# Sums as rows spread by one-hot products, outputs by column halves in turn, input copies ahead of the last exponential, in the state space mixer of a hybrid decoder step

## The reference, cut to what matters

```python
acs = jnp.cumsum(dt * a.reshape(G, J), axis=2)
...
seg = acs[:, :, :, None] - acs[:, :, None, :]
decay = jnp.exp(jnp.where(causal, seg, -jnp.inf))
cb = jnp.einsum('bclgn,bcsgn->bclsg', cc, bc)
y_diag = jnp.einsum('bclsg,bclsgj,bcsgjp->bclgjp', cb, decay, xdt)
...
y_off = jnp.einsum('bclgn,bcgjpn,bclgj->bclgjp', cc, starts, jnp.exp(acs))
```

## Time and profile before

| what | value |
|---|---|
| time before, median of 3 runs | 1987.99 us (1986.82 to 1989.16) |
| the profiled execution | 1985.48 us, span of its trace 1983.7 us |
| TensorE busy | 1925.9 us (97%) |
| VectorE, ScalarE, GpSimd busy | 1252.1, 936.9, 1026.3 us |
| granted clock of TensorE, mean | 0.99 |

### The profile page before, as it was taken

How to read it: one execution, slowest core, us unless ns; L and a number is a source line. 1 busy time by engine, 2 the same in 40 slices (tenths; PEclk the granted TensorE clock), 3 DMA queues, 4 the chain that set the end, 5 groups by cost and what they waited for, 6 DMA issues and landing times.

```text
span 1983.7 us, 35763 instructions
## 1 busy us (share of the span) xinstructions
PE 1925.9 (97%) x13954; PEld 1737.1 (88%) x13954; DVE 1252.1 (63%) x2224; ACT 936.9 (47%) x1573; POOL 1026.3 (52%) x1249
## 2 busy tenths in 40 slices
PE   7999999998999999999999999999999999999997
PEld 5999989798888988788889999999997889889976
DVE  5888343426887788764246888888455158874452
ACT  3676522334565555343345455454342347774333
POOL 4787704036456556232337767677550357675602
PEclk8999999999999999999999999999999999999998
DMA  4444476635344444386454444545487344445860
GB/s 136 147 143 151 139 245 234 213 107 176 111 133 133 133 139 148 112 307 213 141 169 151 132 141 146 153 147 162 142 307 244 107 138 147 133 155 177 278 228 27
DMA packets 332615, 324.64 MB, mean 164 GB/s; under 512 B 19768, under 2 KB 313056, under 8 KB 332448
## 3 DMA queue, kind: packets, MB, share of 16 engines
q1 hardware_dynamic: 330944, 321.49, 50.9%
q10 hardware_dynamic: 1504, 0.87, 0.2%
HBM read 292.16 MB, written 29.61 MB: 162 GB/s over the span
## 4 chain that ended last, share of the span: by engine, by line
PE 61%; DVE 9%; ACT 4%; issue 2%; ACTq 0%; DVEq 0%
PE ps L788 9%; PE ps L793 8%; PE ps L789 8%; PE ps L1487 4%; PE ps L1276 3%; PE ps L1496 2%; PE ps L1553 2%; PE ps L778 2%; PE ps L779 2%; PE ps L780 2%; DVE work L2581 2%; PE ps L1631 1%; PE ps L1570 1%; ACT wh L1742 1%; PE ps L1600 1%
## 5 line engine op out<-in xcount | busy, mean ns | idle before, releaser
L1722 POOL TENSOR_TENSOR wl<-raw,wh 128x256 fp32r<-128x256 f32 x1216 | 1020.8, 874 | 929.6 <-ACT wh L1742 929.4
L1742 ACT ACTIVATE wh<-raw 128x1024 fp32r<-128x1024 f32 x304 | 311.6, 1053 | 164.5 <-PE ps L793 61.8
L788 PE MATMUL ps<-Hh,wh 128*128 128x320 f32 x1200 | 366.3, 319 | 2.3 <-DVE work L2601 0.9
L789 PE MATMUL ps<-Hl,wh 128*128 128x320 f32 x1200 | 354.1, 309 | 0.0
L788 PEld LDWEIGHTS ps<-Hh,wh 128*128 128x128 f32 x1200 | 225.3, 188 | 10.9 <-issue 1.9
L789 PEld LDWEIGHTS ps<-Hl,wh 128*128 128x128 f32 x1200 | 225.5, 188 | 2.2
L2296 DVE TENSOR_SCALAR work<-ps 128x512 f32<-128x512 f32 (+8 forms) x220 | 100.4, 474 | 169.7 <-PE ps L886 40.2
L793 PE MATMUL ps<-Hh,wl 128*128 128x320 f32 x1200 | 200.4, 309 | 0.0
L793 PEld LDWEIGHTS ps<-Hh,wl 128*128 128x128 f32 x1200 | 182.1, 188 | 0.1
L788 PE MATMUL ps<-Oh,wh 128*128 128x320 f32 x512 | 152.3, 311 | 3.7 <-DVE Ol L3048 3.7
L789 PE MATMUL ps<-Ol,wh 128*128 128x320 f32 x512 | 151.2, 308 | 0.0
(11 more groups left out here) (446 smaller groups left out, 3899.0 us busy)
## 6 DMA issues: line engine op xcount, KB each, us to landing
raw<-rg_w_in SPq DMA_DIRECT2D x128, 256.0 KB, 3.6
raw<-hg_w_in SPq DMA_DIRECT2D x128, 256.0 KB, 3.6
raw<-ssd_w_in SPq DMA_DIRECT2D x96, 256.0 KB, 4.0
work<-cache_mem_k SPq DMA_DIRECT2D x40, 512.0 KB, 6.2
work<-cache_mem_v SPq DMA_DIRECT2D x40, 512.0 KB, 4.9
raw<-rg_w_out SPq DMA_DIRECT2D x64, 256.0 KB, 3.6
raw<-x_w_k SPq DMA_DIRECT2D x64, 256.0 KB, 3.7
raw<-x_w_v SPq DMA_DIRECT2D x64, 256.0 KB, 3.8
```

Of the source, the lines that this page charges most:

```text
L788: pe.matmul(ps[:, bank, 0:n], high(half, k), mh[:, k, 0:n], start=(k == 0), stop=False)
L789: pe.matmul(ps[:, bank, 0:n], high(half, k), ml[:, k, 0:n], start=False, stop=False)
L1722: ins = pool.tensor_tensor(out, src, wh[:, parted(n) % HALVES, r:r + 2].bitcast(F32), ALU.subtract)
L1742: act.activation(wh[:, nx.n % HALVES], raw[:, slot, :, half * P:(half + 1) * P], ACT.Copy).then_inc(hi_ready, 1)
```

## The change

Once, in `sums_of_steps`, TensorE also makes the running sums as rows: row 32T + head of a new tile `sd_acs` holds the sums of that head in block T. ScalarE copies them out with two more instructions. `decays(j)` then takes the row of one head and spreads it over 128 partitions by a product with a one-hot column of the identity, repeated 128 times. These products have 32 rows, blocks 0, 1 and 2 in rows 0, 32 and 64 of the array; they go head by head with the three blocks in turn, and all waits for the banks stand ahead of the first.

In `outputs` the two products of each head are ordered so that the two column halves (rows 0 to 63 and 64 to 127 of the bank) alternate; the two products of 64 columns follow.

On ScalarE `take_in(i)` moves ahead of the last exponential of `exps`, and the `ahead(u + 3)` between them goes. On VectorE `last_rows` of the group before moves into `conv`, ahead of its last four instructions.

```diff
+        sd_acs = sb("sd_acs", [96, P])
...
                     for T in range(2):
                         pe.matmul(ps[:, 5, 32 * T:32 * T + 32], upper[:], sd_ta[:, 1, T, :], start=True, stop=True)
                         pe.matmul(ps[:, 5, 96 + 32 * T:128 + 32 * T], later[:], sd_ta[:, 1, T, :], start=True, stop=True)
+                        pe.matmul(ps[32 * T:32 * T + 32, 5, 256:384], sd_ta[:, 1, T, :], upper[:], start=True, stop=True)
                     pe.matmul(ps[:, 5, 192:224], ones[:], sd_ta[:, 1, 1, :], start=True, stop=True)
                     pe.matmul(ps[64:P, 5, 64:96], s_causal[64:P], sd_ta[64:P, 1, 2, :], start=True, stop=True)
+                    pe.matmul(ps[64:96, 5, 256:320], sd_ta[64:P, 1, 2, :], s_causal[64:P], start=True, stop=True)
...
                 def decays(j):
-                    def dta(T, h, n, rows=slice(0, P)):
-                        return sd_ta[rows, 1, T, 4 * j + h:4 * j + h + 1].broadcast_to([rows.stop - rows.start, n])
-
-                    for T, bank, read in ((0, 4, "sd_xt_read"), (1, 5, "sd_xs_read")):
-                        pe.wait_ge(*past(read, j + 1))
-                        for h in range(4):
-                            mm = pe.matmul(ps[:, bank, h * P:(h + 1) * P], dta(T, h, P), upper[:], start=True, stop=True)
-                        mm.then_inc(S(f"sd_seg{T}_full"), 1)
+                    pe.wait_ge(*past("sd_xt_read", j + 1))
+                    pe.wait_ge(*past("sd_xs_read", j + 1))
                     pe.wait_ge(*past("sd_bt_read", j + 1))
+                    for h in range(4):
+                        for T in range(3):
+                            rows, w, c = slice(32 * T, 32 * T + 32), (P, P, 64)[T], 32 * T + 4 * j + h
+                            one = ident[rows, c:c + 1].broadcast_to([32, P])
+                            mm = pe.matmul(ps[:, 4 + T, h * w:(h + 1) * w], one, sd_acs[rows, 0:w], start=True, stop=True)
+                            if h == 3:
+                                mm.then_inc(S(f"sd_seg{T}_full"), 1)
                     pe.wait_ge(*past("sd_cb_read", j + 1))
-                    for h in range(4):
-                        mm = pe.matmul(ps[:, 6, h * 64:(h + 1) * 64], dta(2, h, P, sm), s_causal[sm], start=True, stop=True)
-                    mm.then_inc(S("sd_seg2_full"), 1)
...
+                    for T in range(2):
+                        for n in range(2):
+                            h, rows = 2 * t + n, slice(64 * n, 64 * n + 64)
+                            pe.matmul(ps[rows, bank, T * P:(T + 1) * P], sd_xt[:, T, h, :], sd_e[:, T, h, :], start=True, stop=True)
                     for n in range(2):
-                        h = 2 * t + n
-                        rows = slice(64 * n, 64 * n + 64)
-                        for T in range(2):
-                            pe.matmul(ps[rows, bank, T * P:(T + 1) * P], sd_xt[:, T, h, :], sd_e[:, T, h, :], start=True, stop=True)
+                        h, rows = 2 * t + n, slice(64 * n, 64 * n + 64)
                         pe.matmul(ps[rows, bank, 256:320], sd_xt[sm, 2, h, :], sd_e[sm, 2, h, 0:64], start=True, stop=True)
...
                     steps.did(act.activation(w[:, 2, 0:64], ps[:, 5, 0:64], ACT.Copy))
+                    steps.did(act.activation(sd_acs[0:64], ps[0:64, 5, 256:384], ACT.Copy))
+                    steps.did(act.activation(sd_acs[64:96, 0:64], ps[64:96, 5, 256:320], ACT.Copy))
...
                     if j >= 0:
-                        exps(j)
-                    ahead(u + 3)
+                        exps(j, (0, 1, 2), (1, 2))
                     take_in(i)
+                    if j >= 0:
+                        exps(j, (2,), ())
                     ahead(u + 4)
...
                     for k in range(1, 4):
+                        if k == 3 and i:
+                            last_rows(i - 1)
...
                     conv(i)
-                    if j >= 0:
-                        last_rows(j)
                     pack(i)
```

More of the change, by code:

```diff
@@ L1949, in o_high, with exps @@
                     act.activation(Oh[:, o:o + 2, :], sd_y, ACT.Copy).then_inc(S("sd_o_high"), 1)
-                def exps(j):
+                def exps(j, blocks, sums):
                     def of_sums(bank, w, at, n):
@@ L1956, in of_sums @@
                         return act.activation(sd_eo[rows, :, at:at + w], sums, ACT.Exp)
-                    for T in range(3):
+                    for T in blocks:
                         act.wait_ge(*past(f"sd_seg{T}_ready", j + 1))
-                        if T:
+                        if T in sums:
                             steps.did(of_sums(4 + T, (P, 64)[T - 1], (0, P)[T - 1], 0))
                             of_sums(4 + T, (P, 64)[T - 1], (0, P)[T - 1], 1).then_inc(S(f"sd_eo{T}_read"), 1)
+                        if T == 2 and sums:
+                            return
                         rows, w = (slice(0, P), P) if T < 2 else (slice(64, P), 64)
@@ L2044, in ssd @@
                 ahead(u + 2)
-                exps(7)
+                exps(7, (0, 1, 2), (1, 2))
+                exps(7, (2,), ())
                 ahead(u + 3)
```

## The result

The change makes the kernel slower: 1997.27 us (median of 5 runs, 1994.38 to 2000.04) against 1986.82 us for before (5 runs on the same chip), a ratio of 1.0052 (95% interval 1.0038 to 1.0065). That is some 10 us more, and outside the range of the prediction. The profiled execution of after took 1999.43 us, with a span of 1997.7 us.

The account below looks back on a forecast made before the run. TensorE was taken to set the pace of iterations 3 to 6, VectorE's chain that of 1, 2 and 7. -8.1 us without the clock, +6.0 and +0.5 for clock falls, gave -1.6: 1986.4 us, range 1977.5 to 1992.

Parts of the forecast that it names:

- `decays`: TensorE's `decays` with three strips abreast: 1.1 us instead of 2.91, so 1.8 us less an iteration.
- `outputs`: TensorE's `outputs` with column halves abreast: 0.83 us less a call, 1.67 an iteration.
- start of VectorE's chain: VectorE's first subtractions in `decays`: block 0 ready 0.1 us later, line 2626 1.2 us behind the start of `decays`.
- d: Delay of block 0's end in `decays`: 0.1 us if strips run abreast; rival, in a row, 1.3, +7.5 us, chance 0.10.
- VectorE's chain: From `decays` to the second read of the outputs: stays at 25.4 us, change 0, bounds -0.4 to +0.4 an iteration.
- Copies: Earlier ScalarE input copies: `take_z(i,0)` can go at 633.05 instead of 634.4; TensorE waits 0.4 us, without the move 1.8.
- Once, in iteration 1: ScalarE's two sum copies +0.5 us; `decays` after all three reads, at the lower clock, +0.3; +0.8 in all.
- Iterations 1, 2 and 7: TensorE's pauses for `gate` at their ends grow to 3.2 us; clock falls there cost 2.0 us each, +6.0.
- Iteration 8: VectorE waits for TensorE, so both `outputs` calls count, -1.7 us; a clock fall there takes 0.5 back.
- Iterations 3 to 6, "1.85 of it pass until the fourth `gains` waits for VectorE: 4 x 1.8 = -7.2": TensorE can come 1.85 us earlier in each before the fourth `gains` waits for VectorE's output read: -7.2 us.
- One of the prediction's own signs of being wrong: `gains` not waiting for VectorE's line 2670 would mean that VectorE's chain moved with TensorE.
- a rival with 0.07 and 4 us for two falls: The clock also falls inside iterations 3 to 6 at TensorE's new waits: two falls, +4 us, 1990.4 us, chance 0.07.

Follow-up runs that it names:

- x2: Before with only the row sums, their two copies and the one-hot `decays`; 1989.91 us, 1.0014 of before.
- x3: Before with only the new order of the products in `outputs`; 1992.68 us, 1.0028 of before.
- z3: After with 12 products that nobody reads ahead of each of iterations 2, 3 and 8; 1988.75 us, 1.0007 of before.
- z1: y4 with ScalarE's two splits, `ahead(u + 4)`, behind `states` instead of ahead of it; 1978.92 us, 0.9953 of before.
- x1: Before with the new tile `sd_acs` alone, unused; 1986.58 us, 1.0001 of before.
- y4: After with `gate` ahead of `outputs` in iterations 1, 2, 7, last two `gains` behind `take_bc`, `first_out` and `add_out` earlier; 1978.81 us, 0.9954 of before.
- y1: After with `first_out` ahead of `squares_of` in iterations 3 and 4, and VectorE's first `add_out` ahead of `outputs(j, 1)`; 1990.91 us, 1.0012 of before.

## Why the prediction was wrong

- *`decays`, `outputs`, start of VectorE's chain*: right. 1.09 us (1.1 forecast), 0.83 less a call (0.83), VectorE 1.19 us behind (1.2). The strips run abreast, and d was 0.1. *VectorE's chain*: right, 25.3 us instead of 25.4 (0 forecast). *Copies*: right in that `take_z(i,0)` would wait all of the 1.8 without the move (1.72 in x2); with it the wait is 0.19 us (0.4 forecast). The 0.62 us for `states` in each iteration of after was not foreseen. The move alone was not tried.
- *Once, in iteration 1*: +0.8 forecast, not borne out. ScalarE's copies of the sums take 1.38 us in all instead of 1.13, +0.3 and not +0.5. VectorE begins `decays` 4.50 us behind the first transpose instead of 5.53 before (5.33 in x3, where the clock was up), so earlier and not 0.3 later.
- *Iterations 1, 2 and 7*: right in kind. Pauses of 3.25 us (3.2), the clock fell behind all three, and by z3 that cost 2.50, 2.76 and 1.39 us, 6.65 in all (6.0). That the sum came out so near is partly luck: a fall was priced at 2.0 for 6.7 us at the low clock. The windows above give (1 - 0.72) x 12/0.5 = 6.7 us in 1 and 2, which cost more than 2.0, and (1 - 0.86) x 12/0.5 = 3.4 in 7, half as long.
- *Iteration 8*: -1.2 forecast. The distance to before shrinks by 2.1 us from its transposes to 871 us.
- *Iterations 3 to 6, "1.85 of it pass until the fourth `gains` waits for VectorE: 4 x 1.8 = -7.2"*: this step failed; it came out as +3.3. It failed twice over. One of the prediction's own signs of being wrong says so: in after the `gains` of iterations 3 to 6 wait for nothing.

First, the slack (how much earlier TensorE could come before something held it up) was not 1.85 us, since another wait binds sooner than that of `gains`. The rows of before that say so, timeline of ScalarE and TensorE in iteration 4, and of VectorE in 5:

```profile
653.65 0.47 ACT L1987 ACTIVATE work<-work 128x320 f32<-128x320 f32 x1 [1.90 <-DVE work L2675]
654.03 0.75 ACT L1992 ACTIVATE work<-ps 128x320 f32<-128x320 f32 x2
...
655.50 0.42 PE L778 MATMUL ps<-Oh,wh 128*128 128x320 f32 x1
...
700.72 0.88 DVE L2701 TENSOR_TENSOR work<-work,ps 128x320 f32<-128x320 f32 x2
```

ScalarE's `first_out` (line 1992) stands behind its second square, which waits for VectorE, and ends at 654.78. The second `take_out`, 655.50, can come only 0.7 us earlier. In iterations 5 and 6 `add_out` ends at 701.60, and the second `take_out` stands at 655.50 + 46.95 = 702.45: 0.85 us. With the clock up, z3 saved 46.95 - 46.45 = 0.50 and 46.96 - 46.07 = 0.89. So 1.35 and 0.96 us of the 1.85 were never there, 4.6 us in the four.

In after the same chain, timeline of VectorE and ScalarE, iteration 4:

```profile
664.05 0.53 DVE L2680 SCALAR_TENSOR_TENSOR work<-work,smallc,ps 128x320 f32<-128x320 f32 x1
...
665.54 0.47 ACT L1993 ACTIVATE work<-work 128x320 f32<-128x320 f32 x1 [1.90 <-DVE work L2685]
665.91 0.74 ACT L1998 ACTIVATE work<-ps 128x320 f32<-128x320 f32 x2
```

It ends at 666.65, and `take_out` starts at 666.80.

Second, the clock fell in all four, 1.5 us each, 6.1 in all. The prediction had this as a rival with 0.07 and 4 us for two falls, and set it aside because "each wait lies between long projections". But these waits lie right behind all four `gains`, over 2 us of products that use 32 rows of the array, where the pauses of 0.90 us in before lie behind two. That this decides it was not tried, and other traces speak against so simple a rule. The pause at the end of iteration 7 in x2 is that of before, 0.91 us behind two `gains`, and the clock fell behind it. In z1 it fell at a pause of 0.60 us behind two `gains` in iteration 2, and stayed up at one as long in iteration 1. The timeline and a window around it, first of x2, then of z1, and the window of z1's other pause:

```profile
795.94 0.41 PE L779 MATMUL ps<-Oh,wh 128*128 128x320 f32 x1 [0.91 <-DVE gate_area L2604]
792.00:804.00 12.00, 10.67 (x51) 7.71 (x49) 9.74 (x20) 5.07 (x8) 3.15 (x4) 0.86 0.46 144
...
565.25 0.50 PE L789 MATMUL ps<-Hh,wh 128*128 128x320 f32 x1 [0.60 <-DVE work L2610]
562.00:574.00 12.00, 11.40 (x63) 8.91 (x62) 11.05 (x22) 6.16 (x10) 6.19 (x6) 0.86 0.16 50
523.00:535.00 12.00, 11.39 (x74) 8.90 (x73) 11.26 (x23) 6.48 (x10) 6.51 (x6) 1.00 0.15 48
```

So what decides whether the clock falls at a short wait stays open. The Trainium skill (TensorE: Matmul & The Clock Gate, section A second HAM failure mode: psum-queue depth-cycling) tells of a kernel in which short idle times between groups of products came often enough to make the clock swing between its levels. The rows of after agree, with waits of 1.04 and 0.68 us and a clock of 0.79 around each.

4.6 + 6.1 = 10.7 us accounts for what lies between the forecast of -1.6 and what after's mixer shows. From the first transposes on, after loses 6.6 + 3.3 - 2.1 = 7.8 us, and 1.0 between 448 us and these transposes, 8.8 in all, where -1.6 + 10.7 is 9.1. That 1.0 is no more than single executions differ: x1 has the code of before there and takes 0.8 us longer than before over the same stretch. The profiled executions differ by 4.7 us more ahead of 448 us, which is scatter as well (x1).

## What to carry to other kernels

When an engine gets faster, list every wait that it would come to earlier, copies of other engines that free its buffers too, and take the smallest slack; an engine that was always late shows no waits in its profile, so their sizes must be read from when the releaser ended. A faster TensorE beside engines that keep their pace can make the kernel slower, because its waits lower its clock; then the orders of the other engines have to move with it (y4: 8.5 us under before), and products that nobody reads, in the waits, show at once whether the clock is the cause.

## What the runs showed of the hardware

The clock fell around a wait of only 0.34 us (y1, iteration 5) and of 0.68 us (after), both at four `gains` of 32 rows, while a pause of 0.90 us in before, behind two of them, left it at 1.00. Neither the length of the wait nor the products ahead of it decide alone: it fell at 0.91 us behind two `gains` in x2 and at 0.60 in z1, and in one execution of z3 it stayed up at a wait of 1.05 us and fell at one of 1.04 us an iteration later. A fall cost an iteration 1.4 to 1.5 us where the windows give 3.4 us at the low clock, and 2.5 to 2.8 where they give 6 or more.
